# One decoder trunk on one core: LayerNorm halves for ScalarE, turned x first, spatial sums moved to a tail

## What is computed

```
def layer_norm(x, g, b):
    mu = mean(x); var = mean(square(x - mu))
    return (x - mu) * rsqrt(var + 1e-5) * g + b

def chunked_spatial_gating(x, w_in, v_ln_g, v_ln_b, w_s, s_bias, w_out):
    u, v = split(gelu(x @ w_in), 2)
    v = layer_norm(v, v_ln_g, v_ln_b)           # then 8 heads, chunks of 128 positions
    s = einsum("hts,bcshd->bcthd", tril(w_s), v) + s_bias
    return (u * s) @ w_out

def moe(x, ...):
    scores = sigmoid(x @ router_w); biased = scores + router_bias
    # 8 groups of 8 experts; the 4 groups with the best sum of two; of these the best 8 experts
    gate = scores[top8] / sum(scores[top8]) * 2.5
    y = sum over the 8 of gate * (silu(x @ w_gate[e]) * (x @ w_up[e])) @ w_down[e]
    return y + (silu(x @ sh_gate) * (x @ sh_up)) @ sh_down

for i in range(2):
    h = gated_short_conv(x, ...) if i == 0 else chunked_spatial_gating(x, ...)
    x = layer_norm(ALPHA * x + h, ln1_g[i], ln1_b[i])
    x = layer_norm(ALPHA * x + moe(x, ...), ln2_g[i], ln2_b[i])
```

## Time and profile before

| | us |
|---|---|
| median of 3 runs | 1288.47 |
| lowest, highest | 1287.94, 1288.66 |
| time of the profiled execution | 1289.11 |
| its span, first to last instruction | 1287.3 |

### The profile page before, as it was taken

One profiled execution on the slowest core, in us unless ns is written; L12 is line 12 of the kernel. 1 busy time (PEld: TensorE's weight loads), 2 busy tenths in 40 slices (PEclk: granted clock), 3 DMA queues, 4 the chain that ended last, 5 costly groups with the idle time before them and its releaser, 6 DMA issues.

```text
span 1287.3 us, 20264 instructions
## 1 busy us (share of the span) xinstructions
PE 1205.8 (94%) x7896; PEld 732.6 (57%) x7896; DVE 566.8 (44%) x1264; ACT 376.9 (29%) x672; POOL 16.2 (1%) x32
## 2 busy tenths in 40 slices
PE   9999999999788888999999999999999898889897
PEld 7986444444234434559999998544444442444454
DVE  5756443333233223327676766634333332332233
ACT  4443221222022222315454444322222220222222
POOL 0001000000000000000000000000000000000000
PEclk9999999999889999999999999999999998999999
DMA  9977999999999999999735435899999999999996
GB/s 302 388 303 314 389 419 416 414 420 421 421 420 422 421 420 421 421 407 401 283 137 194 157 143 238 328 416 416 415 411 421 421 421 420 420 422 420 421 420 260
DMA packets 93937, 473.87 MB, mean 368 GB/s; under 512 B 8336, under 2 KB 23824, under 8 KB 48784
## 3 DMA queue, kind: packets, MB, share of 16 engines
q1 hardware_dynamic: 91776, 469.79, 90.1%
q10 hardware_dynamic: 2064, 2.75, 0.6%
HBM read 471.46 MB, written 1.05 MB: 367 GB/s over the span
## 4 chain that ended last, share of the span: by engine, by line
PE 64%; DMA 25%; SPq 5%; DVE 3%; issue 1%; ACT 1%; POOL 0%; DVEq 0%; ACTq 0%
DMA ring<-in_w_up 24%; PE ps L922 19%; PE ps L794 10%; PE ps L978 7%; PE ps L806 7%; PE ps L844 5%; PE ps L901 4%; PE ps L995 3%; SPq L495 3%; PE ps L934 2%; PE ps L1017 2%; SPq L522 2%; PE ps L1025 1%; PE ps L889 1%; SPq L535 1%
## 5 line engine op out<-in xcount | busy, mean ns | idle before, releaser
L922 PE MATMUL ps<-ring,xsT 128*32 128x512 f32 (+1 forms) x2048 | 328.3, 615 | 50.2 <-DMA ring<-in_w_up 50.0
L922 PEld LDWEIGHTS ps<-ring,xsT 128*32 128x32 f32 (+1 forms) x2048 | 104.6, 124 | 265.1 <-issue 263.6
L1739 DVE SCALAR_TENSOR_TENSOR sig<-sig,slot_gate,ps 128x256 f32<-128x256 f32 x52 | 25.0, 480 | 364.7 <-ACT sig L1374 364.7
L978 PE MATMUL ps<-ring,hidT 128*32 128x512 f32 (+1 forms) x1168 | 182.4, 596 | 2.5 <-DMA ring<-in_w_down 2.1
L1521 DVE TENSOR_TENSOR ring_low<-ring,wh 128x1024 fp32r<-128x1024 f32 (+1 forms) x110 | 126.4, 1149 | 88.0 <-ACT wh L1293 87.1
L1293 ACT CAST wh<-ring 128x1024 fp32r<-128x1024 f32 (+1 forms) x110 | 108.8, 990 | 145.9 <-PE ps L794 61.3
L1762 DVE TENSOR_TENSOR X<-X,ps 128x512 f32<-128x512 f32 x184 | 118.3, 683 | 52.2 <-PE ps L995 37.5
L1374 ACT ACTIVATE sig<-ps 128x256 f32<-128x256 f32 x52 | 20.0, 385 | 402.1 <-PE ps L922 345.5
L1753 DVE TENSOR_TENSOR yl<-ps,yh 128x512 fp32r<-128x512 f32 x104 | 71.6, 691 | 128.8 <-ACT yh L1383 128.8
L1362 ACT ACTIVATE xsT<-ps,cols 128x256 f32<-128x256 f32 x208 | 102.5, 561 | 83.1 <-PE ps L901 83.1
L1383 ACT CAST yh<-ps 128x512 fp32r<-128x512 f32 x104 | 60.6, 587 | 171.4 <-PE ps L978 144.5
(11 more groups left out here) (228 smaller groups left out, 1392.0 us busy)
## 6 DMA issues: line engine op xcount, KB each, us to landing
ring<-in_w_gate SPq DMA_DIRECT2D x124, 1024.0 KB, 20.8
ring<-in_w_up SPq DMA_DIRECT2D x124, 1024.0 KB, 23.6
ring<-in_w_down SPq DMA_DIRECT2D x124, 1024.0 KB, 24.1
ring<-in_b_w_in SPq DMA_DIRECT2D x7, 3072.0 KB, 23.4
ring<-in_b_w_out SPq DMA_DIRECT2D x4, 3072.0 KB, 10.7
ring<-in_a_w_in SPq DMA_DIRECT2D x9, 1024.0 KB, 12.1
ring<-in_w_gate SPq DMA_DIRECT2D x8, 512.0 KB, 24.9
ring<-in_a_w_out SPq DMA_DIRECT2D x1, 3072.0 KB, 18.5
```

What stands on the lines that cost most here:

```text
L922: last = nc.tensor.matmul(ps[first:first + width, p, :], xsT[:, c, p * P + first:p * P + first + width], gate_up_of(layer, k, c), start=(c ...
L978: last = nc.tensor.matmul(ps[first:first + width, 4 + h, :], hidT[:, p, kk * P + first:kk * P + first + width], down_of(layer, k)[:, kk, h ...
```

## The change

- First LayerNorm: VectorE computes the shift (minus mean times reciprocal root) and the first half of X, ScalarE the second half, as the second LayerNorm of layer 0 does already. PE's turn waits for both. The semaphores are shared by all LayerNorms now.
- ScalarE's order behind it: both halves of X, the copies of turned x of tokens 0, then the second four chunks of tokens 1 (`copy_xT1`, taken from VectorE), the scores, and only then the three casts to the high part. PE's filler between the two turns is 4 products instead of 7.
- Spatial sums: `wsT` is loaded by SP behind the last refills of layer 0 (before: ScalarE's queue in mixer 1), masked by POOL ahead of the second LayerNorm of layer 0, multiplied by PE behind the last expert unit of layer 0, with 8 idle products behind instead of 16, and copied by ScalarE in two parts. `wsT` takes another place in SBUF.
- PE reads `over` ahead of the first gate product of the last round; the branch stays at its place.
- Last output pieces: the waits for the last piece's weights and `y` stand behind the products of the piece before it for tokens 0, which are made in one go.

```diff
                 def normalise(t):
                     dve.wait_ge(W.ln_rstd, W.past.ln_rstd + t + 1)
-                    nc.vector.tensor_scalar(X[:, t, :], ps[:, 4 + 2 * t:6 + 2 * t, :].rearrange("p a b -> p (a b)"),
-                                            mv[:, t, 0:1], rstd[:, t:t + 1], ALU.subtract, ALU.mult).then_inc(W.x_ready, 1)
+                    nc.vector.tensor_scalar(shift[:, t:t + 1], mv[:, t, 0:1], rstd[:, t:t + 1], -1.0,
+                                            ALU.mult, ALU.mult).then_inc(W.shifted, 1)
+                    nc.vector.tensor_scalar(X[:, t, 0:HALF], ps[:, 4 + 2 * t, :], mv[:, t, 0:1], rstd[:, t:t + 1],
+                                            ALU.subtract, ALU.mult).then_inc(W.x_ready, 1)
...
+                def copy_xT1():
+                    act.wait_ge(W.xT_done, W.past.xT_done + 4)
+                    for c in range(4, KC):
+                        last = scaled(xT1s[:, c, :], ps[:, 7, (c % 4) * P:(c % 4 + 1) * P], layer, c)
+                    last.then_inc(W.xT_ready, 1)
...
                 nc.scalar.activation(unused[:], minus_half[:], ACT.Sigmoid)
-                copy_high(0, slice(0, KC))
+                for t in range(TT):
+                    act.wait_ge(W.shifted, W.past.shifted + t + 1)
+                    nc.scalar.activation(X[:, t, HALF:D], ps[:, 5 + 2 * t, :], ACT.Identity,
+                                         bias=shift[:, t:t + 1], scale=rstd[:, t:t + 1]).then_inc(W.x_high, 1)
                 act.wait_ge(g.cols_in, 16)
                 copy_xT0(0)
                 copy_xT0(1)
-                copy_high(1, slice(0, KC // 2))
-                copy_high(1, slice(KC // 2, KC))
+                copy_xT1()
                 for t in range(TT):
                     act.wait_ge(W.logits, W.past.logits + t + 1)
                     nc.scalar.activation(score[:, t, :], ps[:, 4 + t, 0:E], ACT.Sigmoid).then_inc(W.scored, 1)
+                copy_high(0, slice(0, KC))
+                copy_high(1, slice(0, KC // 2))
+                copy_high(1, slice(KC // 2, KC))
...
                 keep_clock_up(3, 2)
-                transposes(0, W.x_ready, W.past.x_ready, W.xT_done)
-                keep_clock_up(3, 7)
-                transposes(1, W.x_ready, W.past.x_ready, W.xT_done)
+                for t in range(TT):
+                    pe.wait_ge(W.x_high, W.past.x_high + t + 1)
+                    transposes(t, W.x_ready, W.past.x_ready, W.xT_done)
+                    if t == 0:
+                        keep_clock_up(3, 4)
...
+                    sp.wait_ge(W.sh_gu, W.past.sh_gu + TT)
+                    sp.dma_start(wsT[:], b_wsT).then_inc(g.ws_in, 16)
...
                 pe.wait_ge(W.info_taken, W.past.info_taken + ROUNDS)
+                pe.wait_ge(W.over, W.past.over + 1)
+                more = pe.value_load(over[0:1, 0:1], min_val=0, max_val=1)
                 gate_side(layer, r, 0)
...
                 add_last_unit(1)
-                keep_clock_up(4, 16)
+                if layer:
+                    keep_clock_up(4, 16)
+                else:
+                    pe.wait_ge(B.ws_masked, 1)
+                    for h in range(2):
+                        nc.tensor.matmul(ps[:, h, :], ones[:], wsT[:, 4 * h:4 * h + 4, :].rearrange("p a b -> p (a b)"),
+                                         start=True, stop=True).then_inc(B.sums, 1)
+                    keep_clock_up(4, 8)
...
+                            output(n - 1, 0)
+                            pe.wait_ge(W.wl_ready, n)
+                            pe.wait_ge(A.al_ready if layer == 0 else B.yl_ready, j + 1)
                             for t in range(TT):
                                 for h in range(2):
-                                    output(n - 1, t, (h,))
+                                    if t:
+                                        output(n - 1, t, (h,))
                                     output(n, t, (h,)).then_inc(W.out_done, 1)
```

79 lines of the change are left out of this document (37 added, 42 removed).

## The result

| | before | after |
|---|---|---|
| median, us (runs) | 1288.35 (6) | 1294.62 (6) |
| lowest, highest | 1287.94, 1289.69 | 1293.16, 1295.35 |
| profiled execution: time | 1289.11 | 1295.04 |
| its span | 1287.3 | 1293.3 |
| its mean granted clock | 0.984 | 0.980 |

The ratio after / before is 1.0044, with a 95% interval of 1.0033 to 1.0056: slower by 0.44%, where I forecast no change that can be told, and outside my range. To see where the 6.0 us of span come from, I cut both profiled executions at the same events, each read from a timeline of its engine.

The account below looks back on a forecast made before the run. Three stretches set the time: the chain ahead of the first refill (twice), layer 0's tail and PE's stream in mixer 1. Gains of 4.19 us less losses of 3.88 gave net -0.3, median 1288.2 us, range 1284.4 to 1291.8.

Parts of the forecast that it names:

- Sums: Spatial sums moved from mixer 1 into PE's idle passes behind layer 0's last expert: 1.72 us gained.
- Output pieces: Layer 1: six output products no longer wait for the low half of y, inside PE's stall: 1.41 us gained.
- Router: Behind the first LayerNorm: ScalarE's turned-x copies of tokens 0 are last, so logits come 0.27 us later in each layer.
- Early flag: Tail of layer 0: overflow load moved ahead, branch ends sooner, turn of x starts 1.06 us sooner.
- rival D: Early flag brings nothing, the branch ends where it did: 1289.3 us, or 1285.9 without a meeting; chance 0.14.
- The meeting: Selection: POOL's late subtraction and VectorE's two-input operations exclude each other; `chosen` waits, 1.67 us lost in each layer.
- rival C: POOL first: `masked` stands 2.93 us in both layers, 1290.7 us, up to 1294 with the lower clock; chance 0.20.
- margin of 0.06 us: Selection: the lead by which `masked` was to start before POOL's subtraction, said to be within the error.
- My row for it: Trace end: POOL's one-column operation beside VectorE's product took 1.12 us, other one-column ones 0.55; read as POOL waiting.
- The clock: PE idling some 2.9 us for `chosen` if POOL leads: 1.7 us more for each layer, up to 1294.
- faster: Outcome under 1285.9 us, holding the case without VectorE waiting and half of the flag-brings-nothing case: chance 0.31.
- A: Selection: no meeting, POOL does not hold VectorE up; net -3.6 us, 1284.8 us; chance 0.29.

## Why the prediction was wrong

**Sums, right.** 1.72 forecast, 1.74 measured. The mask ran from 576.90 to 578.00 us, ahead of the sums at 580.23, and ScalarE's copies took 0.59 us each and were done at 582.73, ahead of X at 583.27. Nothing of it was on the path.

**Output pieces, right.** 1.41 forecast and measured. The six products lie inside the stall, and PE still waits 0.30 us behind them.

**Router, right in kind.** 0.27 forecast, 0.19 measured in layer 1 (8.88 against 8.69) and in all profiles where the clock held. As forecast, sharing the LayerNorm won nothing, because ScalarE's copies of the turned x of tokens 0 are last: PE stands 0.33 and 0.23 us for them. For the four copies of tokens 1 it doesn't wait.

**Early flag, wrong.** The 1.06 us were a gain of another edit. My step took a branch time of 2.43 us as a fixed cost that begins when the branch is reached. What the runs show is a stop that ends some 1.45 us after a packet of instructions, whenever the branch begins. Alone the flag won 0.13 us of turn and nothing that can be measured, as rival D had it: the branch ended nearly where it did. The sums' move brought the 1.1 us without the flag, with a branch of 0.25 us that no part of the forecast had. In the changed kernel the gain was then given back by the 1.22 us on issue, so that the tail is 0.35 us longer than before instead of 1.06 shorter: 1.4 us of the miss.

**The meeting, mechanism right, order wrong.** The forecast said that POOL and VectorE exclude each other and put the loss at `chosen`, 1.67 us a layer. With VectorE first it is just that (1.66). But POOL came first, by 0.05 us, and the loss is 2.67 a layer: rival C, which had 2.93. The failed step is my margin of 0.06 us: POOL started 2.49 us behind the end of the router (2.56 forecast), `masked` 2.54 (2.50 forecast). Errors of 0.07 and 0.04 us turned the order. I had named the point; I gave the wrong side of it the higher chance. In layer 1, where the clock held, `masked` came as forecast (2.50) and POOL alone was early (2.44). In all seven kernels with this order of ScalarE's casts POOL was first in both layers, by 0.05 to 0.08 us, so this was no accident. This is 2.0 us of the miss. The Trainium skill (SBUF — State Buffer, Who interferes with whom) states both things that decided here: a VectorE operation with two inputs from SBUF contends with a GpSimd operation that reads SBUF, and the order of issue decides which of them blocks the other. The runs agree for POOL first: 2.96 and 2.06 us, 1.95 for `chosen` when the subtraction was already running, MAX8 unhindered, and no wait beside a fill that only writes. The other side, POOL waiting for VectorE, no run shows. My row for it took 1.12 us in all sixteen profiles beside the same VectorE operation; the 0.55 us that I set against it are those of another operation.

**The clock, undersized and left out of the forecast.** Rival C had 1.7 us more for each layer, from a row of 64 passes that took 5.35 us instead of 3.66 behind a gap of 2.24 us. The size was wrong: the clock stayed low from the first product with `chosen` until late in the gather, some 6 us of work at half speed, and that cost 2.97 us where it came (3.07 and 3.12 in two other profiles). In layer 0 the clock fell elsewhere and cost 0.9. This is 3.9 us, the largest part of the miss.

Together: 2.0 (meeting) + 3.9 (clock) + 1.4 (tail) = 7.3, less 0.16 for the router, 0.6 by which the two DMA stretches were shorter and 0.25 at the start, gives 6.3, the distance between -0.3 and +6.0 us of span. My range ended at 1291.8 although case C reached 1294 by its own sum. I had left 0.12 above the range and should have seen that C with the lower clock holds more: a gap of 2.9 us was its own consequence. The sum for "faster" doesn't close either: A and half of D are 0.29 + 0.07 = 0.36, not 0.31.

One agreement is luck. For the sums, the pieces and the flag together I had 4.19 us, and the kernel with these three took 4.5 us less than the kernel before, run beside it. But the flag's 1.06 us in that sum were won by the sums' move.

## What to carry to other kernels

When an operation is moved on GpSimd, list VectorE's operations in its new window that read two SBUF tensors, and price both orders: if the two starts are within 0.1 us of each other, the worse order belongs into the forecast. A stretch where TensorE waits 2.5 us for a chain of small steps can cost twice, once for the wait and once for the lower clock in what follows: here it was followed by some 6 us of work at half speed, 3.0 us lost, in three of four cases. Idle products that end before the data come prevent it, but in a layer whose clock has already fallen they came on top. A branch that waits for its instructions isn't made shorter by reaching it sooner. And take a bundle apart before you judge it: here the sums and the output pieces were worth 4.5 us with what they brought in the tail, the flag nothing that can be told, and the shared LayerNorm with the late casts cost 10.3.

## What the hardware showed that I had not expected

- VectorE's wait for POOL lies inside the recorded duration of the instruction: a 128x128 operation of 0.29 us is recorded with 2.96 us, one of 16 columns with 2.06. Only a comparison with the same row elsewhere shows it.
- A GpSimd fill of 128x1024 (0.95 us) beside a VectorE operation with two inputs costs VectorE nothing; a GpSimd subtraction of the same tile holds it until it ends (2.67 us of wait in a subtraction of 2.88).
- The branch of PE takes 0.25 to 0.38 us or 2.4 to 3.9 us, and the stop can move to another place of the program, with the same PE program in two kernels at that. In eleven profiles its end lies 1.43 to 1.63 us behind the end of a 16 KB packet of PE's instruction queue.
- The time scatters more where VectorE waits in the selection or the first LayerNorm is shared: 2.2 us between the lowest and the highest for the changed kernel, 4.3 to 6.1 for the six other such kernels with six runs or more, against 1.1 to 2.0 us for the versions with the sums, the pieces, the flag or the empty instructions alone, and 2.4 to 3.8 us for the kernel before in sets of 17 to 21 runs. The losses of clock that come in some profiles and not in others are of this size; that they are the cause of the scatter was not measured for each run.
